# Odd attention of a two-layer trunk: one scale for both softmax maps, squares on ScalarE, another order of steps

## What is computed

```
lam = exp(sum(lp[0] * lp[1])) - exp(sum(lp[2] * lp[3])) + lam_init
s = einsum('bqhcd,bkhcd->bhcqk', qb, k_all)        # c: map 1 and map 2
s = where(qchunk >= kchunk, s, NEG_INF)
p = softmax(s, axis=-1)
a = p[:, :, 0] - lam * p[:, :, 1]
o = einsum('bhqk,bkhd->bqhd', a, v_all)
o = _rmsnorm(o, subln_g) * (1.0 - lam_init)        # over the 128 values of a head
out = o.reshape(B, T, DIFF_W) @ w_out
```

## Time and profile before

| | us |
|---|---|
| median of 3 runs | 2645.36 (2641.21 to 2648.32) |
| the profiled execution, its time | 2651.45 |
| its span | 2649.5 |
| TensorE busy | 2458.7 (93%) |
| VectorE busy | 1714.9 (65%) |
| ScalarE busy | 1194.7 (45%) |
| POOL busy | 117.9 (4%) |
| VectorE busy, 2016 to 2036 us | 18.20 of 20 |
| VectorE busy, 2090.4 to 2117 us | 20.98 of 26.6 |

### The profile page before, as it was taken

One profiled execution on the slowest core, in us unless ns is written; L12 is line 12 of the kernel. 1 busy time (PEld: TensorE's weight loads), 2 busy tenths in 40 slices (PEclk: granted clock), 3 DMA queues, 4 the chain that ended last, 5 costly groups with the idle time before them and its releaser, 6 DMA issues.

```text
span 2649.5 us, 37614 instructions
## 1 busy us (share of the span) xinstructions
PE 2458.7 (93%) x13907; PEld 2197.0 (83%) x13907; DVE 1714.9 (65%) x2819; ACT 1194.7 (45%) x2159; POOL 117.9 (4%) x177
## 2 busy tenths in 40 slices
PE   5999999998899899999989999999997687999998
PEld 4999987976767799988789998777775467999887
DVE  6777647676555877745687774663246858777546
ACT  4445435344344554534555453442233435555444
POOL 1000001100001000000100000100000010000000
PEclk9999999999889999999999999999996889999999
DMA  3333334322203223233432324443251032332335
GB/s 114 90 92 84 98 129 164 104 72 73 76 1 127 64 80 96 80 116 131 150 80 80 96 65 143 139 139 127 68 157 54 1 121 71 90 87 80 109 129 175
DMA packets 259140, 261.89 MB, mean 99 GB/s; under 512 B 25568, under 2 KB 214000, under 8 KB 258977
## 3 DMA queue, kind: packets, MB, share of 16 engines
q1 hardware_dynamic: 254224, 243.83, 30.4%
q0 software_dynamic: 4464, 14.80, 1.6%
q10 hardware_dynamic: 288, 1.10, 0.1%
HBM read 249.11 MB, written 10.58 MB: 98 GB/s over the span
## 4 chain that ended last, share of the span: by engine, by line
PE 77%; DVE 14%; ACT 4%; issue 3%; DMA 1%; POOL 1%; SPq 0%; DVEq 0%; ACTq 0%; POOLq 0%
PE ps L844 12%; PE ps L846 12%; PE ps L845 12%; PE ps L902 5%; PE ps L903 5%; PE ps L904 5%; PE ps L1278 3%; PE ps L1279 2%; PE ps L1280 2%; PE ps L961 2%; PE ps L963 2%; PE ps L962 2%; PE ps L1754 1%; DVE w_all L591 1%; DVE xb L707 1%
## 5 line engine op out<-in xcount | busy, mean ns | idle before, releaser
L844 PE MATMUL ps<-xb,w_all 128*128 128x320 f32 x2400 | 751.2, 313 | 54.7 <-DVE w_all L591 33.9
L845 PE MATMUL ps<-xb,w_all 128*128 128x320 f32 x2400 | 747.9, 312 | 0.0
L846 PE MATMUL ps<-xb,w_all 128*128 128x320 f32 x2400 | 747.8, 312 | 0.0
L844 PEld LDWEIGHTS ps<-xb,w_all 128*128 128x128 f32 x2400 | 456.3, 190 | 62.6 <-issue 46.8
L491 DVE TENSOR_TENSOR w_all<-raw,w_all 128x1024 fp32r<-128x1024 f32 (+1 forms) x204 | 207.9, 1020 | 401.2 <-ACT w_all L501 212.7
L845 PEld LDWEIGHTS ps<-xb,w_all 128*128 128x128 f32 x2400 | 456.4, 190 | 0.0
L846 PEld LDWEIGHTS ps<-xb,w_all 128*128 128x128 f32 x2400 | 456.2, 190 | 0.0
L485 ACT ACTIVATE w_all<-raw 128x1024 fp32r<-128x1024 f32 (+1 forms) x204 | 182.3, 895 | 485.1 <-PE ps L904 260.0
L591 DVE TENSOR_TENSOR w_all<-raw,w_all 128x512 fp32r<-128x512 f32 x404 | 277.8, 690 | 146.9 <-ACT w_all L584 145.9
L584 ACT ACTIVATE w_all<-raw 128x512 fp32r<-128x512 f32 x404 | 253.3, 629 | 182.3 <-PE ps L846 138.9
L902 PE MATMUL ps<-w_all 128*128 128x512 f32 x528 | 205.9, 390 | 0.9 <-DVE w_all L506 0.9
(11 more groups left out here) (355 smaller groups left out, 4002.4 us busy)
## 6 DMA issues: line engine op xcount, KB each, us to landing
raw<-in_w_ffn_out SPq DMA_DIRECT2D x176, 512.0 KB, 3.3
raw<-in_w_ffn_in SPq DMA_DIRECT2D x120, 512.0 KB, 5.0
gain<-in_w_ffn_in SPq DMA_DIRECT2D x56, 512.0 KB, 4.9
raw<-in_w_in_odd SPq DMA_DIRECT2D x56, 256.0 KB, 2.7
raw<-in_w_out_even SPq DMA_DIRECT2D x16, 512.0 KB, 3.5
raw<-in_w_out_odd SPq DMA_DIRECT2D x16, 512.0 KB, 3.4
gain<-in_norm_g POOLq DMA_DIRECT2D x12, 512.0 KB, 7.4
raw<-in_w_in_even SPq DMA_DIRECT2D x24, 256.0 KB, 2.6
```

Source lines behind the costliest of these rows:

```text
L844: nc.tensor.matmul(dst, wl, xh[:, k, :], start=first, stop=False, skip_group_check=True)
L845: nc.tensor.matmul(dst, wh, xl[:, k, :], start=False, stop=False, skip_group_check=True)
L846: mm = nc.tensor.matmul(dst, wh, xh[:, k, :], start=False, stop=(k == HK - 1), skip_group_check=True)
```

## The change

- Lambda and the forget weights' split move: VectorE's product and sum ahead of the parameter copy, ScalarE's exponential and copy ahead of the turned tiles 3 and 4, the rest behind VectorE's own work on tiles 3 and 4.
- The combination is map 1 plus (-lambda x sum 1 / sum 2) x map 2. The ratio is one column; 1 / sum 1 is put on the output of PV, as a factor of the copy into `tok`.
- The sum of squares of a head is one ScalarE instruction of 128 columns with a row sum, issued for step j-4 in iteration j, after the exponentials of j and ahead of the copy of j-2; tile 4's eight heads in iterations 0 to 7. `dve_subnorm` is left with the wait for POOL and the multiplication: tile 4 in iteration 10, tiles 2, 1, 0 in iterations 21, 22 and 34.
- Steps: tiles 2 and 1 by turns for each head, then tile 3 of head h with tile 0 of heads 2h and 2h+1, the last four of tile 3 alone.
- Tiles 0, 1, 2 are turned first and the projection starts on each as it comes; tiles 4 and 3 are turned after its units 1 and 3, and tile 3 is normalised after unit 2's split.

```diff
@@ combine, out (dve_prompt)
-                link(dve, nc.vector.tensor_scalar(p2, p2, rinv[:, 1, r], lamc[:, 1:2], ALU.mult, ALU.mult))
-                nc.vector.scalar_tensor_tensor(p1, p1, rinv[:, 0, r], p2, ALU.mult, ALU.add).then_inc(c_done, 1)
+                link(dve, nc.vector.tensor_scalar(ratio[:, r], rsum[:, 0, r], rinv[:, 1, r], lamc[:, 1:2], ALU.mult, ALU.mult))
+                nc.vector.scalar_tensor_tensor(p1, p2, ratio[:, r], p1, ALU.mult, ALU.add).then_inc(c_done, 1)
...
-                    nc.vector.tensor_copy(tok[:, i, h * P:(h + 1) * P], bank(6 + n % 2, P)).then_inc(o_done, 1)
+                    nc.vector.tensor_scalar(tok[:, i, h * P:(h + 1) * P], bank(6 + n % 2, P), rinv[:, 0, n % 4:n % 4 + 1],
+                                            None, ALU.mult).then_inc(o_done, 1)
@@ steps
-                return [(i * NH + h, i, h) for i in range(NP) for h in range(NH)]
+                order = [(i, h) for h in range(NH) for i in (2, 1)]
+                for h in range(NH):
+                    order += [(NP - 1, h)] + [(0, e) for e in (2 * h, 2 * h + 1) if e < NH]
+                return [(n,) + ih for n, ih in enumerate(order)]
@@ act_prompt
+                if odd and j < NH:
+                    act_square_head(act, NP, j)
+                if odd and j >= d + 2:
+                    n, i, h = st[j - d - 2]
+                    act_square_head(act, i, h, n)
@@ dve_prompt
-                dve_subnorm(dve, NP)
...
-                    if odd and (j - d) % NH == 0:
-                        dve_subnorm(dve, (j - d) // NH - 1)
+                if odd and j == 10:
+                    dve_subnorm(dve, NP)
+                if odd:
+                    for t in COMPLETE[1:NP]:
+                        if j == last_step(t) + d + 5:
+                            dve_subnorm(dve, t)
+        COMPLETE = [NP, 2, 1, 0, NP - 1]
@@ act_square_head
+            sq = nc.scalar.activation(out, tok[:, t, h * P:(h + 1) * P], ACT.Square,
+                                      accum_out=s_ss[:, row, h:h + 1])
+            if h == NH - 1:
+                sq.then_inc(sq_done, 1)
@@ dve_subnorm
-            link(dve, nc.vector.tensor_tensor(sq, tok[:, t, :], tok[:, t, :], ALU.mult))
-            nc.vector.tensor_reduce(s_ss, sq.rearrange("p (h d) -> p h d", d=P), AX.X, ALU.add).then_inc(sq_done, 1)
@@ pe_mix_out
             for k in range(KD):
                 pe_row_unit(pe, u + k, None, k, xt_lhs, TILES[0], k == 0, k == KD - 1,
                             before=free if k == 0 else None, done=m_mm if k == KD - 1 else None)
+                if y == "yO" and k in (1, 3):
+                    pe_turn_y(pe, 3 + k // 2)
+            pe.wait_ge(xt_lo, XT_LO[y] + NT)
@@ dve_mix_out
                 dve_lo(dve, u + i, None, D).then_inc(lo_done, 1)
+                if name == "OO" and i == 2:
+                    dve_subnorm(dve, NP - 1)
+                if name == "OO" and i in (3, 5):
+                    dve_xt(dve, "yO", 3 + i // 4, Y_TURN[3 + i // 4][0])
```

More of the change, by code:

```diff
@@ L227, in build_trunk @@
         h0a = small[:, 320:328]
-        s_ss = small[:, 464:472]
-        s_rs = small[:, 472:480]
+        s_ss, s_rs = view(small, 144, 3, NH), view(small, 168, 3, NH)
+        ratio = small[:, 192:196]
         ident = con[:, C_ID:C_ID + P]
@@ L1200, in pe_xt, with pe_turn_y, xt_src @@
             mm.then_inc(xt_ps, 1)
-        def xt_src(j, c0):
-            at0 = XT_BANK[j] * 512
+        Y_TURN = [(0, 0), (1, 4), (2, 6), (4, 6), (3, 6)]
+        def pe_turn_y(pe, j):
+            t, b = Y_TURN[j]
+            pe.wait_ge(tok_ready, READY["yO"] + COMPLETE.index(t) + 1)
+            if j == 0:
+                pe.wait_ge(p_done, 2 * NSTEP)
+            elif j == 1:
+                pe.wait_ge(pt_done, 2 * NSTEP)
+            elif j == 2:
+                pe.wait_ge(o_done, 2 * NSTEP)
+            else:
+                pe.wait_ge(xt_lo, XT_LO["yO"] + j)
+            for c in range(KD):
+                mm = nc.tensor.transpose(psf[:, b * 512 + c * P:b * 512 + (c + 1) * P], tok[:, t, c * P:(c + 1) * P], ident)
+            mm.then_inc(xt_ps, 1)
+        def xt_src(j, c0, b=None):
+            at0 = (XT_BANK[j] if b is None else b) * 512
             return psf[:, at0 + c0 * P:at0 + D].rearrange("p (c n) -> p c n", n=P)
@@ L1761, in act_prompt @@
             d = BEHIND[odd]
-            for j in range(NSTEP + d):
+            for j in range(NSTEP + d + (2 if odd else 0)):
                 if j < NSTEP:
@@ new lines, in dve_prompt, with last_step, norm_row, act_square_head @@
+                if odd:
[3 more added lines that the diff above has]
+        COMPLETE = [NP, 2, 1, 0, NP - 1]
+        def last_step(t):
+            return max(n for n, i, _ in steps(1) if i == t)
+        def norm_row(t):
+            return t % 2 if t < NP else 2
+        def act_square_head(act, t, h, n=None):
+            row, k = norm_row(t), COMPLETE.index(t)
+            if t < NP:
+                act.wait_ge(o_done, NSTEP + steps(1).index((n, t, h)) + 1)
+                if k >= 3 and h == 0:
+                    act.wait_ge(srs_done, k - 1)
+            at0 = h % 3 * P if t == NP else n % NH * P
+            out = att[:, 3072 + at0:3072 + at0 + P] if t == NP else scratch[:, at0:at0 + P]
+            sq = nc.scalar.activation(out, tok[:, t, h * P:(h + 1) * P], ACT.Square,
+                                      accum_out=s_ss[:, row, h:h + 1])
+            if h == NH - 1:
+                sq.then_inc(sq_done, 1)
@@ new lines, in pool_subnorm @@
+        def pool_subnorm(pool):
+            for k in range(NT):
+                row = norm_row(COMPLETE[k])
+                pool.wait_ge(sq_done, k + 1)
+                nc.gpsimd.tensor_scalar(s_ss[:, row, :], s_ss[:, row, :], 1.0 / P, EPS, ALU.mult, ALU.add).then_inc(gs, 1)
+                pool_count[0] += 1
+                pool.wait_ge(gs, pool_count[0])
+                if k >= 3:
+                    pool.wait_ge(tok_ready, READY["yO"] + k - 1)
+                nc.gpsimd.tensor_tensor(s_rs[:, row, :], s_ss[:, row, :], nhalf.to_broadcast([P, NH]), ALU.pow).then_inc(srs_done, 1)
@@ L2208, in _ @@
             act_mix_begin(act, "OO", 1)
-            for j in range(NT):
-                act_xt(act, "yO", j, (j + NP) % NT)
+            for t in TILES[0]:
+                act_xt(act, "yO", t, t)
             act_mix_out(act, "OO", 4, None)
@@ L2258, in _ @@
             dve_mix_begin(dve, "OO")
-            for j in range(NT):
-                dve_xt(dve, "yO", j, (j + NP) % NT)
+            for t in TILES[0]:
+                dve_xt(dve, "yO", t, t)
             dve_mix_out(dve, "OO", 4, None)
@@ L2304, in _ @@
             pe_prompt(pe, 1)
[L2305 to L2308, removed]
+            for j in range(3):
+                pe_turn_y(pe, j)
             pe_mix_out(pe, "OO", 4, "yO")
@@ L2378, in _ @@
             store("diff_v", vO, v_out)
[L2379 to L2384 removed]
+            pool_subnorm(pool)
             pool_gain_post(pool, 4)
```

55 lines of the change are left out of this document (25 added, 30 removed).

## The result

| | before | changed |
|---|---|---|
| median, runs side by side | 2645.26 (2641.21 to 2648.32, 4 runs) | 2621.95 (2620.06 to 2624.01, 4 runs) |
| the profiled execution | 2651.45 | 2620.06 |
| its span | 2649.5 | 2618.1 |
| first scores to last output of the stage | 106.4 | 93.9 |
| last output to first projection matmul | 16.7 | 5.1 |

The ratio is 0.9913, with a 95% interval of 0.9896 to 0.993: **23.3 us faster**, where 33.1 were forecast. The median lies 10 above the forecast 2612 and inside the range (2603 to 2624). Measured twice more, beside the experiments e5 to e12, the changed kernel had 2614.95 and 2617.48, with ratios of 0.9887 (0.9865 to 0.991) and 0.9905 (0.9883 to 0.9926); all its 16 runs have a median of 2616.4.

What follows compares the result with a forecast made beforehand. TensorE was taken to hold 77% of the chain of waits, VectorE pacing the attention between norm stops. Attention -18.5, hand-over -12.0 and start -2.6 sum to -33.1, taking the median 2645.36 to 2612 us, range 2603 to 2624.

Steps and rivals of the forecast that it cites:

- Steps of tiles 2 and 1: Odd attention: a loop through ScalarE's square, PV and scores paces each pair at 5.18 us; VectorE alone needs 4.34.
- the terms (41.4 + 0.8 - 1.0 + 2.0): Attention start: eight pairs 41.4, tile 4's squares 0.8, first pair without PV -1.0, low clock 2.0 us.
- The arithmetic saved on VectorE buys nothing at full clock: Attention steps: the square lengthens the binding loop, so steps sum to 79.0 us against 76.6 before, +2.4.
- Small prices: Per attention step: ScalarE's square 0.38 us (ends 0.29 and 0.58), VectorE's ratio 0.18, scaled output copy 0.36.
- Last tile-3 steps 3.1 apart: End of the attention: four tile-3 steps take 12.4 us, from a two-step loop of 6.21.
- four groups of one tile-3 and two tile-0 steps about 6.1 each: Attention after the pairs: loops of 4.4, 3.65 and 4.1 us, 12.1 for six steps, 24.4 in all.
- rival B: TensorE's clock stays low through the attention: +25 us, 2637; chance 0.07.
- Norm stops: Attention: four VectorE stops, 22.7 us, give way to multiplications costing 2.4; difference -20.3 us.
- Hand-over: Last attention output to projection: earlier start -11.5, turns inside +1.9, clock regained 2.4; -12.0 us.
- Rival D: Hand-over stays long, projection waiting for tiles or at half clock: half its gain and 3 more lost, 2621; chance 0.12.
- Start: Program start: lambda exponential moved ahead shortens VectorE's wait and TensorE's idle behind it, to 7 us; -2.6 us.
- rival C: ScalarE reloads tables twice per attention step between Square and Exp: 82 us, 2694; chance 0.02.

Runs made afterwards that it cites:

- e5: The changed kernel unedited, measured again as reference on a second chip: 2614.95 us, ratio 0.9887 to the kernel before.
- e12: The changed kernel unedited, measured a third time as reference on another chip: 2617.48 us, ratio 0.9905 to the kernel before.
- e1: Changed kernel with ScalarE's squares moved behind the copy of the turned map: 2611.41 us, ratio 0.9879 to the kernel before.
- e8: Changed kernel with only the norm undone, VectorE squaring and summing 1024 columns and waiting for POOL: 2629.53 us, ratio 0.9952 to the kernel before.
- e4: Changed kernel with only the combination undone (both maps scaled, plain output copy): 2619.63 us, ratio 0.9907 to the kernel before.
- e3: Changed kernel with steps ordered tile by tile (2, 1, 0, 3): 2612.65 us, ratio 0.9881 to the kernel before.
- e11: Changed kernel with the earlier step order (tiles 0, 1, 2, 3) and the square behind the copy: 2604.86 us, ratio 0.9854 to the kernel before.
- e9: Changed kernel with own rows per tile for sums and powers, removing waits that guard shared rows: 2619.74 us, ratio 0.9904 to the kernel before.
- e6: Changed kernel with only the start of the program undone (lambda and forget-weight split late again): 2622.36 us, ratio 0.9917 to the kernel before.
- e7: Changed kernel with all five tiles normalised, turned and split before the output projection: 2627.48 us, ratio 0.9931 to the kernel before.
- e2: Changed kernel with each square of tiles 0 to 3 issued twice: 2624.42 us, ratio 0.9925 to the kernel before.

## Why the prediction was right or wrong

**Steps of tiles 2 and 1: right.** Loop 5.18 forecast, 5.10 measured; without the square 4.80 and 4.81 (e1, e8). Beginning and pairs together, from the first maximum to that of the first tile-3 step, took 42.9; the terms (41.4 + 0.8 - 1.0 + 2.0) give 43.2. That the sum fits so closely is partly luck: the square was put 0.08 too high in each pair, the clock's loss in the second pair was 1.4 for the 2.0 put in, and the multiplication of tile 4, put at nothing, took 0.6. "The arithmetic saved on VectorE buys nothing at full clock" holds for the pairs (e4), not for the last tile-3 steps.

**Small prices.** The square took 0.30, the next instruction of ScalarE starting 0.29 later: the low end of the range, and the estimate that was worked out from the Trainium skill ("VectorE: DVE Perf Modes", section on the TRN2 errata), 0.29, was nearer than my 0.38. The ratio took 0.27 for the 0.18 put in, the output scaling 0.35 for 0.36. So VectorE alone needs 2.89, 2.49, 2.09 and 1.69 a step (e3, e11), 0.12 more than the 2.77, 2.37, 1.97 and 1.57 forecast. "Last tile-3 steps 3.1 apart" was wrong: 2.89. The loop named for them, 6.21, needs tile-3 steps in a row (e3 has them: 6.13); in the change the first PVs there are still of tile 0.

**The failed step: "four groups of one tile-3 and two tile-0 steps about 6.1 each", 24.4, with 2.4 for two multiplications: 26.8. Measured 33.2.** Three things were missing.
- The group. Its mixed loop was put at 6.1 by halving loops over six steps. VectorE alone needs 2.89 + 1.69 + 1.69 = 6.27, and 6.46 was measured at full clock, with the square or without it (e5, e1): 4 x 0.36 = 1.4. The first group took 7.26, 0.8 more; TensorE still turns the last maps of tiles 2 and 1 there and multiplies them with V, which is my reading and not tested.
- The wait of ScalarE for POOL's power, 1.23 us in the chain. It stands in the code of the change, and no term of the sum named it. The second group took 8.88 where 6.46 and a multiplication of 1.2 make 7.66: 1.2; e9 takes the wait away and gains 1.46 there.
- The clock. The third and fourth groups hold no wait for POOL and took 9.20 and 7.82, against 7.66 and 6.46: 1.5 and 1.4 lost, put down to the clock by difference; the third ran at 0.50 throughout, and e5's fourth shows the price without the fall. This is rival B in part: the granted clock was at 1.00 from the third pair to the last and fell in the groups. The Trainium skill ("TensorE: Matmul & The Clock Gate", A second HAM failure mode) tells of clocks that swing between bursts. The pairs, with a pause in each step, did not show it once at 1.00 in the three profiles of the changed kernel and in e9, but e6 and e7, with the same stage code, had one more fall in the third pair, and e2, with two squares in a step, had several (mean 0.88 from 2022 to 2050). The groups showed it in every profile that has them. Which property of the groups brings the fall is open: it is not the wait for POOL nor VectorE's multiplication (e9). Alternating long and short steps is not needed for it, as e3's clock fell in a row of tile-0 steps.

**Norm stops: right in kind.** e8 puts them back and is 14.6 slower. That is the stops less the squares and multiplications that they replace, and not the forecast 20.3 by itself.

**Hand-over: right.** First projection matmul 5.1 us after the last output (5.2 forecast), and 0.87 us of the chain for each of the two turned tiles inside the projection (1.91 forecast together, 1.74). The projection ran at 1.00 from its first matmul. The lead over the kernel before grows by 12.7 from the last output to the end of the projection, forecast 12.0. Rival D falls.

**Start: right.** -3.0 for the -2.6 put in; the wait fell to 6.26, not 7.

**Table loads: none in the stage**, so rival C falls.

The sum by the profiles: -3.0, -12.4 and -12.7, together -28.1, where -2.6, -18.5 and -12.0 were forecast, together -33.1. The term of the groups, 6.4 too low, carries the error; the last tile-3 steps, 1.0 shorter, and the tail behind them, 0.8 longer, nearly cancel. The 4.8 by which the medians differ less than these 28.1 have no cause shown.

## What to carry to other kernels

Where several engines issue in order over two banks, write the loop out for each kind of step, with everything that stands in front on each engine; here it held to 0.1 us, and failed where I guessed a mixed sequence instead. Read every wait that a change adds to protect a shared buffer as a term of the sum. And try the steps that need least of TensorE where its clock is low anyway: of the orders measured, the old one gave the shortest stage, once the rest of the change was there.

## What the runs showed of the hardware that was not expected

- A VectorE operation on one or two columns costs by its form: two scalars from memory 0.27 (L1891), a reciprocal of two columns 0.16 (L1889), one with constants 0.15 (L1196).
- Two squares of 128 columns in a row on ScalarE start 0.29 us apart, although each shows 0.30 and a read of its sum of 0.20: 2048.21, then 2048.50 in e2.
- In the first profile, e5, e9 and e12 TensorE kept 2.4 GHz from the third pair to the last, with a pause in each, and fell to 1.2 GHz at nearly the same step of the second group. e4, e6 and e7 fell at that step too, and once before it in the first group. The 16 runs of the changed kernel differ in their mean granted clock by up to 0.008, and in time by up to 15.6 us.
